# Splitting a memory projection over three normalizations instead of two: the first part runs ahead of the embedding's

## What is computed

```python
mn = rms_norm(mem, mem_norm[l])
mk = rms_norm((mn @ w_mem_k[l]).reshape(B, M, MEM_HEADS, HEAD_DIM), mem_k_gain[l])
mv = (mn @ w_mem_v[l]).reshape(B, M, MEM_HEADS, HEAD_DIM)
```

## Time and profile before

| | |
|---|---|
| median of 3 runs | 2517.68 us (2517.28 to 2517.77) |
| profiled execution, its own time | 2517.68 us |
| its span of instructions | 2515.8 us |
| PE busy | 2503.7 us |
| DVE busy | 1859.9 us |
| ACT busy | 1324.7 us |
| mean granted clock of PE | 1.0 |

### The profile page before, as it was taken

The page is one execution under the profiler, slowest core; times in us unless marked ns, Lnnn a source line. Parts: engine busy times, 40 slices in busy tenths (PEclk is TensorE's granted clock), DMA queues, the critical chain, the costliest instruction groups (busy, mean ns, idle before and its releaser), DMA issues.

```text
span 2515.8 us, 33095 instructions
## 1 busy us (share of the span) xinstructions
PE 2503.7 (100%) x12038; PEld 2103.1 (84%) x12038; DVE 1859.9 (74%) x3004; ACT 1324.7 (53%) x1928; POOL 27.4 (1%) x24
## 2 busy tenths in 40 slices
PE   8999999999999999999999999999999999999999
PEld 7888888888888888888888887888888888888888
DVE  8887668887668777677777786778777767777766
ACT  6676565566566444444444456665544444444443
POOL 4000000000000000000000000000000000000000
DMA  8554556545555555555555554444555555555554
GB/s 312 207 189 170 201 187 232 184 172 180 206 184 186 198 187 198 189 196 192 192 200 178 199 194 150 144 158 174 194 190 194 198 186 187 200 199 192 192 184 151
DMA packets 70847, 479.53 MB, mean 191 GB/s; under 512 B 7872, under 2 KB 10304, under 8 KB 17600
## 3 DMA queue, kind: packets, MB, share of 16 engines
q1 hardware_dynamic: 70720, 477.85, 53.6%
HBM read 474.67 MB, written 2.10 MB: 190 GB/s over the span
## 4 chain that ended last, share of the span: by engine, by line
PE 98%; ACT 0%; DVE 0%; issue 0%; ACTq 0%; DVEq 0%
PE acc L964 14%; PE acc L966 14%; PE acc L965 14%; PE acc L950 12%; PE score L964 10%; PE score L965 10%; PE score L966 10%; PE acc L954 6%; PE score L1337 1%; PE score L950 1%; PE head_ps L1362 1%; PE score L954 1%; PE turn_ps L1346 0%; PE acc L1243 0%; PE acc L1244 0%; PE score L1243 0%
## 5 line engine op out<-in xcount | busy, mean ns | idle before, releaser
L1865 DVE TENSOR_TENSOR low<-raw,high 128x1024 fp32r<-128x1024 f32 (+2 forms) x912 | 1078.1, 1188 | 456.2 <-ACT high L1426 447.6
L1426 ACT ACTIVATE high<-raw 128x1024 fp32r<-128x1024 f32 (+2 forms) x912 | 932.6, 1026 | 845.4 <-PE acc L966 430.4
L964 PE MATMUL acc<-high,xs 128*128 128x512 f32 x928 | 366.2, 395 | 0.4 <-DVE scale_a L1960 0.3
L966 PE MATMUL acc<-low,xs 128*128 128x512 f32 x928 | 361.5, 390 | 0.0
L965 PE MATMUL acc<-high,xs 128*128 128x512 f32 x928 | 361.2, 389 | 0.0
L950 PE MATMUL acc<-xs,high 128*128 128x512 f32 x992 | 325.6, 394 | 0.0
L964 PE MATMUL score<-high,xs 128*128 128x512 f32 x736 | 286.5, 389 | 0.0
L966 PE MATMUL score<-low,xs 128*128 128x512 f32 x736 | 286.3, 389 | 0.0
L965 PE MATMUL score<-high,xs 128*128 128x512 f32 x736 | 286.3, 389 | 0.0
L954 PE MATMUL acc<-xs,low 128*128 128x256 f32 x992 | 244.5, 279 | 0.0
L1914 DVE STREAM_TRANSPOSE unit_turn<-unit_prod 32x128 f32<-32x128 f32 x704 | 212.6, 302 | 9.7
(11 more groups left out here) (429 smaller groups left out, 3386.7 us busy)
## 6 DMA issues: line engine op xcount, KB each, us to landing
raw<-w_up_dram SPq DMA_DIRECT2D x176, 1024.0 KB, 4.8
raw<-w_wide_dram SPq DMA_DIRECT2D x75, 1024.0 KB, 4.8
raw<-w_in_dram SPq DMA_DIRECT2D x64, 1024.0 KB, 4.8
raw<-w_out_dram SPq DMA_DIRECT2D x32, 1024.0 KB, 4.8
raw<-w_heads_dram SPq DMA_DIRECT2D x20, 1024.0 KB, 4.8
raw<-w_mixout_dram SPq DMA_DIRECT2D x16, 1024.0 KB, 4.8
raw<-w_mem_dram SPq DMA_DIRECT2D x8, 1024.0 KB, 4.8
raw<-w_first_dram SPq DMA_DIRECT2D x8, 1024.0 KB, 4.8
```

Source lines behind the costliest of these rows:

```text
L964: eng.matmul(bank_, xh, hi, start=start, stop=False)
L966: return eng.matmul(bank_, xh, lo, start=False, stop=stop)
L1426: eng.activation(high[:, s % SPLIT, to:to + n], raw[:, s % RAW, at_:at_ + n], ACT.Copy).then_inc((highs_a, highs_b)[piece], 1)
L1865: eng.tensor_tensor(low[:, s % SPLIT, w], raw[:, s % RAW, at_:at_ + n], high[:, s % SPLIT, w].bitcast(F32), ALU.subtract).then_inc((lows_a ...
```

## The change

Two slabs of the memory projection (four tiles of the memory, values and keys) become a region `mem0` at the head of `ORDER`, ahead of `lat0`; the six others become `mem1` and `mem2`, three slabs each, in `ln0` and `ln1`. `WARM` is gone. The transfers of the gains, of four memory tiles and of the first slab stand ahead of x, those of the second slab behind the parameters. ACT and DVE prepare memory tiles and slab before the sums of the norm. In `ln0` and `ln1` the turns stand ahead of halves 3, 4 and 5, and turn 3 ahead of row 4 of the next region. ACT copies the first part of the products out of PSUM (`memory_copies`) and later scales the values (`memory_values`); the later two parts are added by DVE.

```diff
+FILL = {"mem0": "emb", "mem1": "ln0", "mem2": "ln1"}
+MEM_CUTS = (0, 4, 10, KT)
```

The sync engine's queue:

```diff
+            eng.dma_start(par[:, 0:KT], t["par"][:, 0:KT]).then_inc(gain_in, 16)
+            eng.dma_start(mem_b[:, 0:MEM_CUTS[1], S:2 * S], t["mem"][:, 0:MEM_CUTS[1], :]).then_inc(mem_in[0], 16)
+            in_halves(0, REG["mem0"], 0)
             for n in range(2 * TB):
...
+            eng.dma_start(par[:, KT:cut], t["par"][:, KT:cut]).then_inc(par_in, 16)
+            in_halves(1, REG["mem0"], 1)
```

The tensor engine: memory slabs, turn 3 in `up10`, turns in the latents, and the start:

```diff
+                elif r.name[:3] == "mem":
+                    rows_ = memory_rows(r.layer)
+                    for piece in range(2):
+                        half = 2 * k + piece
+                        first_turn = 3 if r.layer else 2
+                        if half >= first_turn:
+                            turn_chunk(FILL[r.name], half - first_turn)
+                        piece_ready(piece)
...
+                                if r.name == "up10" and b == 0 and row == 4 and u == 0 and i is None:
+                                    turn_chunk("ln1", 3)
...
-                            if name == "emb" and unit == 0 and b == 0 and row in (2, 4):
+                            if unit == 0 and b == 0 and row in ((2, 4) if name == "emb" else (4,)):
                                 turn_chunk(name, row // 2 + 1)
...
-                    for n in range(WARM):
-                        eng.matmul(sums[:, :], x_tok[:, 0, 0:P], x_tok[:, 0, 0:2 * S], start=True, stop=True)
-                    turn_chunk("emb", 0)
-                    turn_chunk("emb", 1)
```

The scalar engine's `layer_norm`:

```diff
                 if name == "emb":
+                    eng.wait_ge(gain_in, 16)
+                    do("memory", 0, MEM_CUTS[1])
+                    split_high(0, fill, 0, None)
+                    split_high(1, fill, 0, None)
                     whole_squares()
+                    split_high(0, fill, 1, None)
...
                 eng.wait_ge(variance, N_OF[name] + 1)
                 eng.activation(ln_root, ln_var, ACT.Sqrt).then_inc(root, 1)
...
+                    elif j in (2, 4, 6):
+                        split_high(int(j == 4), r, int(j == 6), None)
...
                 if name != "emb":
-                    split_high(0, r, 1, None)
-                    for tile in range(TB, 2 * TB):
-                        natural_out(fill, 3, tile, fill.g0 + 4 * fill.per)
                     split_high(1, r, 1, None)
                 if name == "ln1":
                     for q4 in range(4):
```

The vector engine's `layer_norm`:

```diff
+                if name == "emb":
+                    do("memory", 0, MEM_CUTS[1])
+                    split_low(0, fill, 0, None)
+                variance_of(name, fill)
...
+                    elif j in (4, 6):
+                        split_low(int(j == 4), r, int(j == 6), None)
                     lows_of(name, j)
                 if name != "emb":
-                    split_low(0, r, 1, None)
+                    split_low(1, r, 1, None)
                     for tile in range(TB, 2 * TB):
-                        store(fill, 3, None, tile, 0)
-                    split_low(1, r, 1, None)
+                        store(fill, 2, None, tile, 0)
```

More of the change, by code:

```diff
@@ L40 @@
 TAIL_TILES = 4
-WARM = 4
 LN_EPS, RMS_EPS = 1e-5, 1e-6
@@ L108, in plan @@
         r.s0, r.t0, r.g0 = s, t, g
-        r.spare = int(r.name[:3] == "mem")
+        r.spare = int(r.name[:3] == "mem" and r.tiles > 0)
         s, t, g = s + r.n, t + r.tiles + r.spare, g + r.n * r.groups
@@ L217, with memory_rows @@
 TOGETHER = ("mixout",)
-FILL = {"mem0": "ln0", "mem1": "ln1"}
+FILL = {"mem0": "emb", "mem1": "ln0", "mem2": "ln1"}
+MEM_CUTS = (0, 4, 10, KT)
+def memory_rows(e):
+    n = MEM_CUTS[e + 1] - MEM_CUTS[e]
+    return [(group, at) for group in range(2) for at in range(n)]
 AFTER_NORM = {"emb": "lat0", "ln0": "lat1", "ln1": "up10"}
@@ L256, in layer_steps @@
         put(16, "memory_scale")
+        put(17, "memory_values")
     put(4, "lat_norm", layer, 0)
@@ L283, in layer_steps @@
     put(48 + 12, "moments", ln, 2)
-    for n in range(4):
-        put(48 + 10 + n, "memory", 8 * layer + 2 * n, 8 * layer + 2 * n + 2)
+    for n in range(3):
+        put(48 + 10 + n, "memory", MEM_CUTS[layer + 1] + 2 * n, MEM_CUTS[layer + 1] + 2 * n + 2)
     put(3, "row", layer)
@@ L697, in memory_tile @@
         def memory_tile(n):
-            return mem_b[:, n % 8, S:2 * S], memh[:, n % 8, :], p_("mem_g", n), mem_in[n // 8]
+            e = sum(n >= cut for cut in MEM_CUTS[1:])
+            at_ = n - MEM_CUTS[e]
+            return mem_b[:, at_, S:2 * S], memh[:, at_, :], p_("mem_g", n), mem_in[e]
         def in_mix(r):
@@ L900, in slot @@
                     eng.wait_ge(lows_b, val(s - RAW + 1, 4, i))
[L901 to L905, removed]
+                if i is None and s < RAW:
+                    if s >= 2:
+                        in_halves(s, r, k)
                 else:
@@ L1066, in slot @@
                     latents(r, k)
+                elif r.name[:3] == "mem":
[6 more added lines that the diff above has]
+                        piece_ready(piece)
+                        for b in range(TB):
+                            for c, (group, at_) in enumerate(rows_[2 * half:2 * half + 2]):
+                                tile, end = TB * group + b, at_ == len(rows_) // 2 - 1
+                                a = bank_free(tile, 0) if at_ == 0 else bank_of(r, tile)
+                                w = slice((2 * piece + c) * 512, (2 * piece + c + 1) * 512)
+                                if b == 0:
+                                    eng.wait_ge(mem_l, MEM_CUTS[r.layer] + at_ + 1)
+                                last = product_natural(a, memh[:, at_, :], high[:, pos_, w], low[:, pos_, w], b, at_ == 0, end)
+                            if b == 0 and end:
+                                last.then_inc(first_half if r.layer else memory_half, 1)
+                        last.then_inc(products, 1)
                 elif r.kind == "unit":
@@ L1619, in layer_norm, with memory_copies @@
                         eng.activation(square[:, 4 * q4:4 * q4 + 4, :], x[:, 4 * q4:4 * q4 + 4, :], ACT.Square).then_inc(squared, 1)
+            def memory_copies(fill, group):
+                for b in range(TB):
+                    if b == 0:
+                        eng.wait_ge(memory_half, group + 1)
+                    else:
+                        eng.wait_ge(products, fill.g0 + 2 * group + 2)
+                    eng.activation((memv, stage)[group][:, b, :], bank_of(fill, TB * group + b), ACT.Copy).then_inc(memory_out, 1)
             def second_scaled(name, c):
@@ L1658, in do @@
                     eng.activation(mem_rooted[:, 8:10], mem_variance[:, 8:10], ACT.Sqrt).then_inc(mem_root, 1)
+                elif kind == "memory_values":
+                    eng.wait_ge(mem_scaled, 1)
+                    for b in range(TB):
+                        eng.activation(memv[:, b, :], memv[:, b, :], ACT.Copy, scale=mem_inv[:, 8 + b:9 + b]).then_inc(memory_valued, 1)
                 elif kind == "memory_heads":
                     b = a[0]
-                    eng.wait_ge(stored, REG["mem1"].t0 + 2 * TB)
+                    eng.wait_ge(stored, REG["mem2"].t0 + 2 * TB)
                     for n in range(MEM):
@@ L1960, in store @@
                         done(eng.tensor_scalar(to, from_, token[:, 2, b:b + 1], None, ALU.mult))
-                    elif r.name == "mem0" and tile < TB:
-                        done(eng.tensor_scalar(to, from_, mem_inv[:, 8 + b:9 + b], None, ALU.mult))
                     else:
```

107 lines of the change are left out of this document (47 added, 60 removed).

## The result

The changed kernel takes 2525.82 us (median of 7 runs, 2524.19 to 2528.78), the kernel before 2517.39 (7 runs, 2517.14 to 2517.97): ratio 1.0034, 95% interval 1.0024 to 1.0044, slower by 8.4 us. The forecast was 2523.6 with a range up to 2528. The profiled execution took 2526.33 us, its span is 2524.5, so 8.7 us above that of before.

What follows compares the result with a forecast made beforehand. PE's unchanged work, plus time PE does nothing useful, was taken as the bound. Front -0.9, ln0 +1.45, ln1 +5.25 and `memory_values` +0.1 made +5.9 us on 2517.68: 2523.6 us, range 2518.5 to 2528.

Steps and rivals of the forecast that it cites:

- PE is the bound and its work stays the same: Whole kernel: PE is full everywhere but at the start, 98% of the chain, and the change leaves its work.
- ln0: new wait 1.45: In ln0, PE waits 1.45 us for piece 1 of lat1's slab 1, behind turn 3; bounds 0.5 to 2.5.
- ln1: 1.9 and 3.35: In up10, new waits of 1.9 us at slab 1 and 3.35 at slab 2, together 5.25; bounds 3.9 and 7.
- The front gives 0.9 us: At the start, empty PE time falls from 15.1 to 14.2 us, a gain of 0.9, not 10.9.
- z and not slab 0 sets the start: At the start, PE is through slab 0 by 16.7 and waits 2.8 us for z, at 18.4.
- Warming products: nothing in the sum: At the start, removing four warming products costs slab 0 1.9 us at most, ended before z: 0 in sum.
- The gaps bring the array back to 1.2 GHz: Rival, 12%: gaps of 2.8 us at the start and 3.35 in ln1 each cost up to 1.9: 2525.5 to 2527.4.
- The later norms do not wait: Rival, 12%: waits of ln0 and ln1 together stay under 0.9 us, only the front counts: 2516.8 us.
- the front at its best: Rival, 4%, on top of no later waits: PE full from 9.7, 2514.2 us, or 2512.3 without half pace.
- transfers 2 us slower: Rival, 8%: at the start, transfers in the new order take two us more: 2525.6 us.
- `memory_values` 0.1: In uq0, two ACT copies of 0.62 us each cost PE 0.1 us, 0.6 at most.

Runs made afterwards that it cites:

- experiment 3: Changed kernel with slab 1's second halves taken early in lat1 and up10, and both halves of up10's slab 2 ahead of squares and adds: 2518.75 us.
- experiment 1: Changed kernel with the second half of slab 1 of lat1 and up10 moved directly behind the first half on ScalarE and VectorE: 2524.16 us.
- 2: Changed kernel with only the first half of up10's slab 2 taken ahead of the squares on ScalarE and the adds on VectorE: 2524.27 us.
- experiment 4: Changed kernel with five fp32 products of a tile of zeros put ahead of the first memory product: 2526.44 us.
- 6: Changed kernel with only the start reordered: slab halves interleaved with x's parts in the transfers, ScalarE and VectorE order changed to match: 2525.37 us.
- experiment 7: Changed kernel with all the moves of experiment 3 together with the reordered start of 6: 2516.87 us.
- 8: Kernel of experiment 7 with the five products of zeros put ahead of the first memory product: 2517.96 us.
- the second filler kernel: Repeat run of the changed kernel with twelve unused 512-column products in the wait ahead of up10's slab 2: 2525.41 us.

## Why the prediction was right, and which terms were off

It said slower, by new waits in the later norms; the time of 2525.82 lies in its range, 2.2 above its point. By its own steps:

- **PE is the bound and its work stays the same.** Right: experiment 3 takes the waits away and nearly all of the loss goes with them.
- **ln0: new wait 1.45.** Measured 1.4 to 1.55, on piece 1 of `lat1`'s slab 1, and taking that half out from behind turn 3's chain removes it (experiment 1).
- **ln1: 1.9 and 3.35.** Measured 1.9 and 3.2, at the halves named. That the second hangs on squares and adds is shown by 1 (it grows when the first goes) and 2 (it goes when it is put ahead of them).
- **The front gives 0.9 us.** Wrong sign: it costs 0.4. The term that was mis-sized is the landing of the slab's halves, put at 6.9 and 8.1; ScalarE's copies could begin at 8.22 and 9.52 (in the earliest of eight executions at 7.58 and 8.89). The memory tiles were as forecast (copies from 5.34 on, forecast 5.6). The estimate lined the transfers up behind each other, 1.25 apart, from the tiles on. The two halves and x's first part do come 1.3 apart, but half 0 itself came 2.9 behind the tiles. By then the transfer engines had moved more than what was queued up to it, as the section on the hardware shows. So turn 0 came at 20.43, not 19.5, `lat0` at 27.95, not 26.9, and the product that started at 32.26 before starts at 43.53: 0.4 more than the two slabs' 10.88, where the forecast had 0.9 less. The step that z and not slab 0 sets the start held (4, 6, 7).
- **Warming products: nothing in the sum.** Right. Restored, they moved turn 0 by 0.03 us. The products they would have quickened did run at half pace, 0.43 us apart until 15.45. The Trainium skill's page "TensorE: Matmul & The Clock Gate", section "What's actually happening", says that a cold array runs at half rate until it has been busy for a while, and these rows agree. In this place the price is hidden behind z. The price itself was put too low: slab 0 takes 2.3 us more than in experiment 4, where the forecast had 1.9 at most from the earlier trace rows.
- **The gaps bring the array back to 1.2 GHz (12%, up to 1.9 us each).** This rival came true for one of its two gaps, at 1.7 us, and with the front's sign makes the difference: 5.9 + 1.3 (front) + 1.7 is 8.9, against 8.7 measured in the span. The argument against it was a gap of 1.8 us that did nothing, and the gaps forecast were 2.8 and 3.35; the row spoke for short gaps only. The gap at the start, forecast at 2.8, was 1.8. Its own terms give less than 2.8: 9.7 + 5.44 + 1.9 is 17.0 and not 16.7, so 2.5; the rest is the longer half pace. Where it did come out at 2.4 or more (experiments 1, 4, 8 and the second filler kernel) the clock fell there too. That this rival's 2525.5 lies next to the measured 2525.82 is luck in part: it has the start 1.3 too cheap, and with the start as measured it would have said 2526.8.
- **The later norms do not wait; the front at its best; transfers 2 us slower.** The first two did not happen. The third did in part: the halves were 1.3 to 1.4 late, the norm 0.9, the tiles not at all.
- **`memory_values` 0.1.** Measured nothing. The two copies run at 121.8 and 122.4, 0.71 us each. The start's 0.4 is already complete at 43.53 and is still 0.4 in `ln0`, so no time is lost between. In the trace of the changed kernel:

```profile
43.53 0.50 PE L1282 MATMUL acc<-high,xs 128*128 128x512 f32 x1
```

```profile
L1698 ACT ACTIVATE memv<-memv,mem_stat x2: 712/712/712, 121.8 to 122.4; 128x512 f32<-128x512 f32 x2
```

The point of the forecast missed by 2.2 us, and that is two terms: the start (+1.3) and the clock. In the timed runs the clock's part is about 1.6 us of the 8.4, as far as one run can say: the only one at 1.000 took 2524.19, which is 6.8 above the kernel before. Two other kernels close the account at full clock: the five such runs of experiment 3 lie 0.4 above the kernel before, which is the start, and experiment 7 lies 0.8 below it, which is the start in its new order (span 0.9 less).

## What to carry to other kernels

When work that covers others' latency is moved away, look at what stood behind it on the helper engines, and look there for idle time ahead of the late piece: here 3 us of it lay unused directly ahead of 5 us of new waits, and reordering gave back 7 of 8 us. Move the whole run of late pieces, not the first: each move alone passed a part of its gain to the next piece. And an idle array costs more than its idle time: price a forecast gap against the nearest gap of the same length in the trace, and do not take a short gap that did no harm as evidence for a longer one. Where a kernel's times fall into two groups, look at the clock of each run before comparing medians.

## What the runs showed of the hardware

The waits of PE for z at the start and for slab 2 in `up10`, with the granted clock behind them, in the profiled executions of all these kernels: waits of 0.2 to 1.9 us were followed by 1.00 (fourteen of them, the one of 1.77 in the kernel before among them); waits of 2.38, 2.46, 2.60, 3.05, 3.05, 3.10, 3.10, 3.83 and 4.13 us by a stretch at half pace, every time. Except in experiment 4 the stretch took 1.7 us of work, 3.4 us at 1.2 GHz, whether the wait was 2.4 or 3.8 us long. In experiment 4 both stretches were 6.8 us long: at the start the three windows lose 0.10 x 4 + 0.50 x 4 + 0.25 x 4 = 3.4 us of clock, which is 6.8 us at 1.2 GHz, the last 1.3 us of the wait among them; in `up10`, behind a wait of 3.05, the products are at half pace from 784.64 to 790.35, 3 us of work. Why is open.

The length of a wait does not decide alone. In experiments 4 and 8 the array stood idle for 2.57 and 2.29 us between the products of zeros and slab 0, and slab 0 then ran at full pace (10.93 and 11.16 in experiment 4's rows). What sets that gap of 2.57 apart from the waits of 2.38 and more was not tested.

At the very start the granted clock does not show half pace. In the changed kernel it reads 1.00 over a window whose products start 0.43 us apart, so the pace there was read from the starts:

```profile
12.00:16.00 4.00, 4.00 (x12) 3.10 (x11) 3.93 (x7) 2.55 (x5) 0.00 (x0) 1.00 1.03 414
```

The landing of a transfer could not be worked out from its place in the queue. Half 0 of the slab could be used 6.6 us after the start of its issue when it stood directly behind the tiles, and 6.3 us after it when 512 KB of x stood between. The same order of transfers gave 7.58 to 7.76 in three executions and 8.22 to 8.28 in five. A window of the changed kernel up to the copy of half 0 says something of why a place in the queue is not enough:

```profile
0.00:8.22 8.22, 0.00 (x0) 0.00 (x0) 1.74 (x5) 3.19 (x7) 0.19 (x4) 1.00 0.70 218
```

218 GB/s over 8.22 us are 1.79 MB, and gains, tiles and half 0 together are 1.06 MB. The other 0.7 MB belong to transfers queued behind it, so these were under way before half 0 could be used. What shares the rate out among them, and what makes the two groups, is open.
